# A state-space stage in four-pair blocks, its rotation sum moved to GpSimd, and feed-forward banks opened by their first products

## The reference

```python
dt = jnp.exp(f32(log_dt))[:, None]
mag = jnp.exp(lr * dt)
ar, ai = mag * jnp.cos(li * dt), mag * jnp.sin(li * dt)
...
bur = jnp.einsum('lbgh,gph->lbgp', uc, bbar_re)
bui = jnp.einsum('lbgh,gph->lbgp', uc, bbar_im)
_, _, sr, si = lax.associative_scan(_complex_affine_combine, (a_r, a_i, bur, bui), axis=0)
xr = pr * xr0 - pi_ * xi0 + sr
xi = pr * xi0 + pi_ * xr0 + si
y = jnp.einsum('ghp,lbgp->lbgh', cr, xr) - jnp.einsum('ghp,lbgp->lbgh', ci, xi)
...
y = y.transpose(2, 0, 1, 3, 4).reshape(Bsz, S, G * H) + f32(d_skip) * f32(u)
g = jax.nn.gelu(y).astype(u.dtype)
val, gate = jnp.split(g @ w_glu + b_glu, 2, axis=-1)
```

## Time and profile before

| What | us |
|---|---|
| plain runs, median of 3 | 3118.63 (3114.32 to 3121.56) |
| profiled execution, its own time | 3114.8 |
| span of its trace | 3112.5 |
| TensorE busy | 2954.6 (95%) |
| VectorE busy | 694.2 (22%) |
| ScalarE busy | 411.3 (13%) |
| GpSimd busy | 445.9 (14%) |

### The profile page before, as it was taken

One profiled execution on the slowest core, in us unless ns is written; L12 is line 12 of the kernel. 1 busy time (PEld: TensorE's weight loads), 2 busy tenths in 40 slices (PEclk: granted clock), 3 DMA queues, 4 the chain that ended last, 5 costly groups with the idle time before them and its releaser, 6 DMA issues.

```text
span 3112.5 us, 48823 instructions
## 1 busy us (share of the span) xinstructions
PE 2954.6 (95%) x21703; PEld 1865.3 (60%) x21703; DVE 694.2 (22%) x1237; ACT 411.3 (13%) x808; POOL 445.9 (14%) x320
## 2 busy tenths in 40 slices
PE   5999999979989999999999898989999999999999
PEld 2876788834475565556555433534444444898888
DVE  2304210076530000000001285310000012351000
ACT  0032010010111000000000343310000011121000
POOL 0014009456500000000000072000000000240000
PEclk7999999977799999999999897999999999999999
DMA  8576464437736999999998210012222222222442
GB/s 279 151 269 240 140 168 150 150 130 258 252 117 238 376 370 378 382 381 378 381 384 303 91 54 14 14 57 79 81 71 71 75 71 78 95 68 68 149 155 87
DMA packets 363784, 564.40 MB, mean 181 GB/s; under 512 B 43684, under 2 KB 196300, under 8 KB 363468
## 3 DMA queue, kind: packets, MB, share of 16 engines
q1 hardware_dynamic: 341436, 556.79, 51.4%
q10 hardware_dynamic: 22160, 4.77, 0.8%
HBM read 557.31 MB, written 1.05 MB: 179 GB/s over the span
## 4 chain that ended last, share of the span: by engine, by line
PE 51%; issue 34%; POOLq 5%; POOL 2%; DMA 2%; DVE 2%; ACT 1%; SPq 1%; DVEq 1%; ACTq 1%
PE psum L749 11%; PE psum L1396 10%; PE psum L1272 5%; PE psum L1412 5%; POOLq L2680 3%; PE psum L796 3%; PE psum L865 2%; PE psum L1438 2%; PE psum L1020 2%; DMA prow<-in_s_log_dt 1%; PE psum L778 1%; POOLq L2770 1%; PE psum L1465 1%; PE psum L1069 1%; PE psum L1354 1%
## 5 line engine op out<-in xcount | busy, mean ns | idle before, releaser
L1141 PE MATMUL psum<-ring,xe 128*32 128x256 f32 x8448 | 465.7, 380 | 0.0
L749 PE MATMUL psum<-act_in,ring 128*128 128x256 f32 x1920 | 422.4, 381 | 7.6 <-DVE act_in L1973 3.3
L749 PEld LDWEIGHTS psum<-act_in,ring 128*128 128x128 f32 x1920 | 366.0, 191 | 60.3 <-DVE act_in L1973 3.4
L1141 PEld LDWEIGHTS psum<-ring,xe 128*32 128x32 f32 x8448 | 269.7, 110 | 182.6 <-issue 8.4
L1396 PE MATMUL psum<-a,ring 128*128 128x512 f32 x704 | 304.6, 596 | 8.7 <-DVE a L2478 8.7
L1165 PE MATMUL psum<-ring,zs 128*32 128x256 f32 x4224 | 238.4, 381 | 4.2 <-ACT zs L1757 4.2
L1396 PEld LDWEIGHTS psum<-a,ring 128*128 128x128 f32 x704 | 134.5, 191 | 178.3 <-issue 178.3
L1272 PE MATMUL psum<-a,ring 128*128 128x512 f32 (+1 forms) x480 | 211.5, 603 | 4.8 <-ACT a L1795 4.1
L1165 PEld LDWEIGHTS psum<-ring,zs 128*32 128x32 f32 x4224 | 139.0, 110 | 94.9 <-issue 5.9
L2416 DVE TENSOR_TENSOR zs<-zs,psum 128x128 f32<-128x128 f32 x132 | 37.8, 288 | 643.4 <-ACT zs L1753 643.2
L1272 PEld LDWEIGHTS psum<-a,ring 128*128 128x128 f32 (+1 forms) x480 | 91.8, 192 | 122.8 <-issue 120.8
(11 more groups left out here) (391 smaller groups left out, 3075.5 us busy)
## 6 DMA issues: line engine op xcount, KB each, us to landing
ring<-in_moe_w SPq DMA_DIRECT2D x320, 512.0 KB, 7.0
ring<-in_ffn_w SPq DMA_DIRECT2D x98, 1024.0 KB, 5.2
ring<-in_ada_w SPq DMA_DIRECT2D x96, 1024.0 KB, 7.1
ring<-in_moe_w SPq DMA_DIRECT2D x88, 1024.0 KB, 8.7
ring<-in_hg_w_in SPq DMA_DIRECT2D x20, 1024.0 KB, 5.0
ring<-in_mlstm_w_in SPq DMA_DIRECT2D x16, 1024.0 KB, 5.6
ring<-in_moe_w SPq DMA_DIRECT2D x64, 256.0 KB, 5.6
ring<-in_mlstm_w_out SPq DMA_DIRECT2D x8, 1024.0 KB, 6.5
```

Source lines behind the costliest of these rows:

```text
L749: last = pe.matmul(bank(j)[:, n * T:(n + 1) * T], tile[:, k * width + n * P:k * width + (n + 1) * P], src(k), start=start and k == 0, stop ...
L1141: last = pe.matmul(psum[32 * g:32 * g + 32, r, 0:2 * P].rearrange("p (u n) -> p u n", u=2), xe[:, 2 * i + k, at:at + 32], tile[:, k, :, g ...
```

## The change

The state-space stage now works in blocks of four pairs with four buffers. `drive_two` issues the input products of two pairs on neighbouring row groups. VectorE's `products` are a step of their own and run one pair ahead of `scan`; their sum, `rotation_sum`, is GpSimd's. `turn_back` leaves out the subtraction and the addition: the four products go to TensorE as they are, and `read_out` does sixteen matmuls a block, four terms over four column groups, with signed copies of C (`cmT`, `c_re_neg`). Parts of the buffers of pairs 2 and 3 are used for input and output, so the next block waits for `s5_y_full` there. The three modulation steps of a block stand around the read-out. `ada_columns` becomes four transposes in this stage; ScalarE copies what is needed of each (`mod_cols_out`), and VectorE reduces all of it at the end. B and C are turned inside feed-forward 0, ahead of its last two groups of products, and copied by ScalarE; GpSimd applies signs and the parity mask. `clear_sums` goes: the first down products open their banks with the start flag. The loops of TensorE's feed-forwards are written out.

```diff
@@ -202,12 +202,12 @@
  ("ffn3", 3 * FSTEPS)]
-("m_out", 4), ("ln0", 4), ("ffn0", 2 * FSTEPS), ("ln1", 4), ("s_bT", 4), ("s_cT", 4),
+("m_out", 4), ("ln0", 4), ("ffn0", 2 * FSTEPS - 2), ("s_bT", 4), ("ffn0_last", 2), ("s_cT", 4), ("ln1", 4),
...
@@ -417,8 +421,12 @@
-zris, ztmp = (xrows[:, 0:2], xrows[:, 2:4]), xrows[:, 10:12]
-xris, xtmp = (xrows[:, 4:6], xrows[:, 6:8]), xrows[:, 8:10]
+xparts = (xrows[:, 4:8], xrows[:, 12:16], zs[:, 0:4], zs[:, 4:8])
+zris = (xrows[:, 0:2], xrows[:, 2:4], xparts[2][:, 0:2], xparts[3][:, 0:2])
+ztmps = (xrows[:, 8:10], xrows[:, 10:12], xparts[2][:, 2:4], xparts[3][:, 2:4])
+ctok_flat = ctok.rearrange("p a b c d -> p (a b c d)")
+c_re_neg = ctok_flat[:, 0:DC * P].rearrange("p (c s) -> p c s", s=P)
+mods_raw = ctok_flat[:, DC * P:DC * P + 24 * 32].rearrange("p (s m n g) -> p s m n g", s=24, m=4, n=2)
...
@@ -772,6 +780,12 @@
+        if stage == "c":
+            if s:
+                pe.wait_ge(S("mod_cols_out"), s)
+            for m in range(4):
+                last = pe.transpose(psum[:, 7, m * P:(m + 1) * P], mod_rows[:, m * P:(m + 1) * P], ident)
+            return last.then_inc(S("mod_cols_full"), 1)
...
@@ -844,27 +860,22 @@
-    def clear_sums():
-        for b in range(4):
-            pe.matmul(psum[:, NB + b, :], zeros[:], cst[:, 0:BANK],
-                      start=True, stop=False, skip_group_check=True)
+        def down(t, i, last_step=False):
+            wait_tile(pe, t)
+            wait_out(pe, step_job(name, i) + 1)
             for n in range(DC):
                 for k in range(2):
                     last = pe.matmul(psum[:, NB + n // 2, (n % 2) * T:(n % 2 + 1) * T],
                                      ring[:, t % RING, k * D + n * P:k * D + (n + 1) * P],
-                                     hid[:, i % 2, k], start=False, stop=last_step and k == 1,
+                                     hid[:, i % 2, k], start=i == 0 and k == 0 and n % 2 == 0,
...
+        for i in range(steps - 1):
+            t, j = t0 + 2 + 3 * i, step_job(name, i + 1)
+            if before_last is not None and i == steps - 2:
+                before_last(0)
+            mm_pair(t, j, lambda k: act_in[:, k])
+            mm_pair(t + 1, j + 1, lambda k: act_in[:, k])
+            down(t + 2, i)
+        if before_last is not None:
+            before_last(1)
+        down(t0 + 3 * steps - 1, steps - 1, True)
...
@@ -1027,50 +1041,67 @@
+        def turn_b_or_c(which):
+            if which == 0:
+                pe.wait_ge(S("bpad_ready"), 1)
+                for g in range(4):
+                    turn(job_of["s_bT"] + g, [bpad[:, g // 2, 4 * (g % 2) + i] for i in range(4)])
+            else:
+                pe.wait_ge(S("s5_in"), 9 * 16)
+                for g in range(4):
+                    turn(job_of["s_cT"] + g, [ctok[:, g // 2, 4 * (g % 2) + i].rearrange("p d s -> p (d s)")
+                                              for i in range(4)])
+        ffn("ffn0", FSTEPS, lambda k: pe.wait_ge(S("ffn0_in_ready"), k + 1), turn_b_or_c)
         layer_norm(1, lambda g: pe.wait_ge(S("ln_sum_ready"), g + 1))
...
-        wait_out(pe, job_of["s_cT"] + 3)
-        def drive(p):
-            c, r = p // 4, 32 * (p % 4)
-            j = job_of["s_pair"] + p
-            wait_free(pe, j)
-            if r == 0:
+        wait_out(pe, job_of["s_bT"] + 3)
+        def drive_two(b):
+            c = b // 2
+            for p in (2 * b, 2 * b + 1):
+                wait_free(pe, job_of["s_pair"] + p)
+            if b % 2 == 0:
                 pe.wait_ge(S("s5_u_ready"), c + 1)
             for i in range(2):
-                last = pe.matmul(bank(j)[:, i * T:(i + 1) * T], bT[r:r + 32, i, c], act_in[r:r + 32, c],
-                                 start=True, stop=True)
-            full(last, j)
-        drive(0)
-        drive(1)
-        for p in range(NPAIR):
-            if p + 2 < NPAIR:
-                drive(p + 2)
-            c, r = p // 4, 32 * (p % 4)
-            pe.wait_ge(S("s5_x_ready"), p + 1)
-            if p % 4 == 0 and c >= 2:
+                for p in (2 * b, 2 * b + 1):
+                    r, j = 32 * (p % 4), job_of["s_pair"] + p
+                    last = pe.matmul(bank(j)[:, i * T:(i + 1) * T], bT[r:r + 32, i, c], act_in[r:r + 32, c],
+                                     start=True, stop=True)
+                    if i:
+                        full(last, j)
+        def read_out(c):
+            pe.wait_ge(S("s5_x_ready"), 4 * c + 4)
+            if c >= 2:
                 pe.wait_ge(S("s5_y_out"), c - 1)
-            for i in range(2):
-                last = pe.matmul(psum[r:r + 32, NB + c % 2, 0:T], cmT[:, i, c, r:r + 32], xris[p % 2][:, i],
-                                 start=i == 0, stop=i == 1)
-            last.then_inc(S("s5_x_used"), 1)
-            if p % 4:
-                ada_step("c", 3 * (p // 4) + p % 4 - 1, 1, 2)
+            terms = ((cmT[:, 0], 0), (c_re_neg, 2), (cmT[:, 1], 1), (cmT[:, 1], 3))
+            for n, (held, part) in enumerate(terms):
+                for i in range(4):
+                    r = 32 * i
+                    last = pe.matmul(psum[r:r + 32, NB + c % 2, 0:T], held[:, c, r:r + 32], xparts[i][:, part],
+                                     start=n == 0, stop=n == 3)
+            last.then_inc(S("s5_y_full"), 1)
+        drive_two(0)
+        drive_two(1)
+        pe.wait_ge(S("cmT_ready"), 1)
+        for c in range(DC):
+            if c + 1 < DC:
+                drive_two(2 * c + 2)
+            ada_step("c", 3 * c, 1, 2)
+            if c + 1 < DC:
+                drive_two(2 * c + 3)
+            ada_step("c", 3 * c + 1, 1, 2)
+            read_out(c)
+            ada_step("c", 3 * c + 2, 1, 2)
         ada_end("c", 2)
...
@@ -1686,15 +1720,42 @@
+        def b_out():
+            for g in range(4):
+                j = job_of["s_bT"] + g
+                wait_full(act, j)
+                out_of(act.activation(bT[:, g // 2, 4 * (g % 2):4 * (g % 2) + 4],
+                                      bank(j).rearrange("p (c s) -> p c s", s=P), ACT.Copy), j)
+        silu_steps("ffn0", FSTEPS, s5_exponentials, b_out)
+        for g in range(4):
+            j = job_of["s_cT"] + g
+            wait_full(act, j)
+            out_of(act.activation(cmT[:, g // 2, 4 * (g % 2):4 * (g % 2) + 4],
+                                  bank(j).rearrange("p (c s) -> p c s", s=P), ACT.Copy), j)
         layer_norm(1)
...
+        def mod_cols_out(s):
+            act.wait_ge(S("mod_cols_full"), s + 1)
+            turned = psum[:, 7].rearrange("p (m g x) -> p m x g", m=4, g=4)[:, :, 0:2]
+            act.activation(mods_raw[:, s], turned, ACT.Copy).then_inc(S("mod_cols_out"), 1)
+        for s in range(24):
+            if s:
+                mod_cols_out(s - 1)
+            mod_rows_out("c", s)
+            if s >= 3 and s % 3 == 1:
+                gelu(s // 3 - 1)
+        mod_cols_out(23)
+        gelu(DC - 1)
...
@@ -2265,64 +2327,66 @@
-        def pair(c, i):
+        def products(c, i):
             p = 4 * c + i
             j = job_of["s_pair"] + i
-            dve.drain()
             dve.wait_ge(bank_full[j % NB], c + (j // NB + 1))
             b = halves_of(bank(j).rearrange("p (k t) -> p k t", k=2))
-            zri = zris[i % 2]
-            z, zt = halves_of(zri), halves_of(ztmp)
+            z, zt = halves_of(zris[i]), halves_of(ztmps[i])
             sin = turn(1, p)
-            if not (isinstance(c, int) and i < 2):
-                dve.wait_ge(S("s5_x_ready"), p - 1)
+            if not isinstance(c, int):
+                if i < 2:
+                    dve.wait_ge(S("s5_x_ready"), p - 3)
+                elif i == 2:
+                    dve.wait_ge(S("s5_y_full"), c)
             dve.tensor_tensor(zt[:, 0], b[:, 1], sin[:, 0], ALU.mult)
             dve.scalar_tensor_tensor(zt[:, 1], b[:, 0], -1.0, sin[:, 0], ALU.mult, ALU.mult)
             out_of(dve.tensor_tensor(z, b, turn(0, p), ALU.mult), j)
-            dve.drain()
-            dve.tensor_tensor(zri, zri, ztmp, ALU.add)
-            dve.drain()
+        def scan(c, i):
+            p = 4 * c + i
+            dve.wait_ge(S("s5_sum_ready"), p + 1)
             mag_t = sv[:, 3, bass.ds(p, 1)].broadcast_to([P, SL])
             for k in range(2):
-                last = dve.tensor_tensor_scan(zri[:, k], mag_t, zri[:, k], 0.0, ALU.mult, ALU.add)
+                last = dve.tensor_tensor_scan(zris[i][:, k], mag_t, zris[i][:, k], 0.0, ALU.mult, ALU.add)
             last.then_inc(S("s5_z_ready"), 1)
         def y_out(c, back):
             c = c + back
-            dve.wait_ge(S("s5_x_used"), 4 * c + 4)
+            dve.wait_ge(S("s5_y_full"), c + 1)
             dve.scalar_tensor_tensor(gT[:, bass.ds(c, 1), :], act_in[:, bass.ds(c, 1), :],
                                      par[:, bass.ds(prow_at["s5_d"] + c, 1)],
                                      psum[:, bass.ds(NB + c % 2, 1), 0:T], ALU.mult, ALU.add
```

(58 more changed lines are left out.)

79 lines of the change are left out of this document (31 added, 48 removed).

## The result

The kernel after takes 3083.36 us (median of four, 3077.72 to 3088.78), the kernel before beside it 3117.98; the ratio is 0.9889 [0.9866, 0.9911], so 34.6 us less, give or take 7. The forecast was 3084.1 and 34.5 us less.

A forecast was written before the change was run, and what follows sets the result against it. It took the state-space stage as bound by a chain of waits, no engine full. Stage -35.5, added transposes +3.6 and cleared banks -2.6 gave -34.5 us: 3118.63 to 3084.1, range 3061 to 3104.

The forecast's parts named there:

- The block, forecast at 20.5 us: State-space stage: four pairs at 4.95 us on GpSimd, 19.8 us, plus 0.7 net waiting for the read-out.
- Start, and transposes ahead of it: State-space stage's first products 7.4 us earlier; 32 added transposes before the last feed-forward products cost 3.6 us.
- No engine is full: Old state-space stage, 655 to 845 us: VectorE, GpSimd and transfers each about 70% busy, so waits bind it.
- at the lower clock it never idles, which is when it rose before: State-space stage: at 1.2 GHz TensorE would have no idle time, so its clock should rise; argued against rival 2.
- rival 2: State-space stage: TensorE becomes the bound at 1.2 GHz, blocks 21.6 us, total 3096, up to 3105; chance 22%.
- the discount for the clock: Two feed-forwards without zero matmuls: a falling clock gives back 1 to 3 us, so -1.3 each, not -2.8.
- VectorE is no longer the full engine: New state-space stage: VectorE needs only 3.6 to 4.4 us a pair, scans 2.1 to 2.9 of it.
- GpSimd, forecast as full at 4.95: New state-space stage: GpSimd's three operations take 4.95 us a pair, 3.8 alone, slowed by sharing with VectorE.
- The upper bound of 5.1 us a pair: State-space stage: GpSimd and VectorE exclude each other wholly, 3.8 us plus 1.27 of scans alone.
- The barrier at 0.7 us net: Between state-space blocks: GpSimd stands 1.0 or 2.7 us for the read-out, scans fill part, 0.7 us remains.
- The term of the pairs: State-space block: four pairs at 4.95 us on GpSimd make 19.8 us, ends 17.6 and 20.5.
- Tail: Last read-out to the GLU products: 6.4 us at the higher clock, 10.7 at the lower, taken as 9.

The follow-up runs named there:

- second profile of after: The kernel after, unchanged, run and profiled again: median 3083.16 us, ratio to before 0.9912.
- The form without a barrier: Kernel after with each block's read-out done pair by pair and buffers freed per pair: median 3063.77 us, ratio to before 0.9832.

## Why the prediction was right

The total was right; of its terms about half were. By its own steps, against the second profile of after, which, like that of before, has no stall (it was also the fastest of its four executions, 5.9 us under their median, so the sum is a little flattering):

| Step | forecast | measured |
|---|---|---|
| zero matmuls, first place | -1.3 | -2.6 |
| first feed-forward, with 32 transposes | +3.6 | +2.9 |
| layer norm 1 to the first rotation products | -7.4 | -7.3 |
| those to the GLU products | -28.1 | -28.2 (202.0 to 173.8 us) |
| GLU products to the last feed-forward | 0 | +0.8 |
| zero matmuls, second place | -1.3 | -2.7 |
| sum | -34.5 | -37.1 |

The block, forecast at 20.5 us, is 20.9 in this profile.

- Start, and transposes ahead of it: right in mechanism and size. The two groups of 16 transposes push the products behind them by 1.75 us each, 3.5 together against 3.6; the table shows 2.9 because the feed-forward also starts with less waiting, as told above.
- "No engine is full", read from a mean over the stage of before: wrong for its two long blocks, in which TensorE was full at the lower clock, 29.9 of 29.9 us. And "at the lower clock it never idles, which is when it rose before", the argument against rival 2, doesn't hold for them: with TensorE busy without a gap from 710 on, the clock stayed at 0.50 beyond 730. The forecast lost nothing by it, since the new stage was set against the whole old one, long blocks included, but it didn't see where most of the gain would come from: in the traces of after TensorE, with less to do, holds nobody up within a block.
- Zero matmuls: the step that failed was the discount for the clock. The delay was read rightly from the earlier trace rows, 2.8 us; the clock did fall, but in a stretch in which TensorE waits for VectorE, so it gave nothing back. The full term was the right one.
- "VectorE is no longer the full engine", 3.6 to 4.4 us a pair: wrong. Without a barrier it is busy all the time at 4.46 a pair. The scans were taken at 2.1 to 2.9 us and mostly take 3.2 to 3.4, and VectorE goes without a gap until the barrier. GpSimd, forecast as full at 4.95, has 4.5 a pair to do (1.27 + 1.39 + 1.65 and 0.2 between) and waits 0.74 us for scans at two pairs of a block. The price of sharing was booked mainly on GpSimd, and most of it falls on the scans: they grow by 2.0 us (1.27 to 3.3), GpSimd's three operations by 0.5. The upper bound of 5.1 us a pair assumed that nothing overlaps; 4.46 shows that some does.
- The barrier at 0.7 us net: too small. The form without a barrier measures 17.8 a block against 20.8, so the barrier costs 3.0 us, with the lower clock of its read-out in it. I had the read-out at 2.0 or 3.7 (measured 3.4, at the lower clock) and let later scans fill the wait, but the work that could fill it stands behind it on both engines. The term of the pairs was 2.0 us a block too high (4 x 4.95 = 19.8 against 17.8), this one 2.3 too low. The block came out right because they cancel.
- TensorE: input products of two pairs side by side take 1.13 us at the higher clock (701.42 above), so row groups do overlap, as I had taken. The rival with TensorE as the bound was wrong for after in its premise that the clock stays low: the steps over the weights take 1.90 us, as at 1.00, and the clock is 0.50 at each read-out, after 7 us without work. It was right that the clock costs something: 1.5 us a block.
- Tail: 7.9 us from the fourth turn-back's end (814.27) to the first GLU product (822.14) in the first profile, forecast 9, ends 6.4 to 10.7. In the second profile, too, it is 7.9: 1.1 too much was forecast here, and 1.2 too little from the first sum to the last turn-back (641.37 to 805.83).
- Not foreseen at all: the stall of about 7 us in the first feed-forward, in some executions. It is in before's family too (6.6 us in the kernel without zero matmuls), and the load that causes it costs both kernels something, before more (8.5 us against 4.9), so the difference of the medians (-34.6) lies between the two profiled ones (-28.7 and -37.1) and holds some of it.

So the forecast was closer than it deserved: two errors of 2 us a block cancelled, and the missing 2.7 us of the zero matmuls don't show in the medians. How often the stall falls into the executions of each kernel isn't known. That the medians came out 0.1 us from the forecast is luck: a repetition gave 31.8, and 28 without the load of small pieces on both sides.
